# The scores of two attention steps issued together, and the turns of a step ahead of every product with V

## What is computed

```python
for layer in range(DEPTH):
    h = _rmsnorm(x, mix_norm_gain[layer])
    proj = h @ w_in[layer].astype(h.dtype)
    q, k, v, conv_in = jnp.split(
        proj, [ATTN_WIDTH, 2 * ATTN_WIDTH, 3 * ATTN_WIDTH], axis=-1)
    ...
    q = _rope(_rmsnorm(q, q_norm_gain[layer]), cos, sin)
    k = _rope(_rmsnorm(k, k_norm_gain[layer]), cos, sin)
    attn = _dilated_attention(q, k, v).reshape(b, s, ATTN_WIDTH)
    ...
    mix = jnp.concatenate([attn, u], axis=-1)
    x = x + mix @ w_out[layer].astype(mix.dtype)
    ...
    x = x + (jax.nn.silu(gate) * val) @ w_down[layer].astype(h.dtype)
```

## Time and profile before

| | |
|---|---|
| median of 3 runs | 2282.95 us (2280.68 to 2283.87) |
| profiled execution, its own time | 2281.74 us |
| its span | 2280.0 us |
| PE busy | 2237.1 us, 98% |
| DVE busy | 1791.0 us, 79% |
| ACT busy | 950.4 us, 42% |
| attention stage, layer one | about 246 to 371 us of the span |
| attention stage, layer two | about 1378 to 1503 us |

### The profile page before, as it was taken

One profiled execution on the slowest core, in us unless ns is written; L12 is line 12 of the kernel. 1 busy time (PEld: TensorE's weight loads), 2 busy tenths in 40 slices (PEclk: granted clock), 3 DMA queues, 4 the chain that ended last, 5 costly groups with the idle time before them and its releaser, 6 DMA issues.

```text
span 2280.0 us, 31670 instructions
## 1 busy us (share of the span) xinstructions
PE 2237.1 (98%) x11160; PEld 1852.5 (81%) x11160; DVE 1791.0 (79%) x2259; ACT 950.4 (42%) x1454; POOL 150.4 (7%) x65
## 2 busy tenths in 40 slices
PE   8999999999999999999999999999999999999999
PEld 6888788887888888888788887888878888888887
DVE  5999885688777777778849998856887777777785
ACT  5323685444333333333432237845533333333331
POOL 0131002100000000000102210021000000000000
PEclk9999999999999999999999999999999999999999
DMA  4324640101111111111212246401011111111112
GB/s 160 103 84 120 167 112 11 65 19 56 39 54 55 55 55 55 55 55 37 93 47 83 75 129 178 92 20 56 19 56 56 56 41 51 55 55 55 55 39 109
DMA packets 47980, 158.25 MB, mean 69 GB/s; under 512 B 7568, under 2 KB 10256, under 8 KB 47888
## 3 DMA queue, kind: packets, MB, share of 16 engines
q1 hardware_dynamic: 47024, 154.64, 21.6%
q10 hardware_dynamic: 864, 2.36, 0.3%
HBM read 135.74 MB, written 21.23 MB: 69 GB/s over the span
## 4 chain that ended last, share of the span: by engine, by line
PE 87%; DVE 8%; issue 1%; ACT 1%; DMA 1%; DVEq 0%; SPq 0%; ACTq 0%
PE mm L600 34%; PE aux L611 20%; PE mm L611 17%; PE mm L697 4%; PE aux L773 4%; PE aux L755 3%; PE mm L728 3%; PE aux L636 1%; DMA w_raw<-weights 1%; DVE cv L1895 1%; DVE y L1595 1%; DVE t_all L1941 1%; DVE ring L1873 1%; DVE x_lo L1825 1%; DVE ring L1505 0%
## 5 line engine op out<-in xcount | busy, mean ns | idle before, releaser
L600 PE MATMUL mm<-x_hi,ring 128*128 128x512 f32 x1536 | 498.6, 390 | 4.5 <-ACT uv L1336 2.9
L611 PE MATMUL aux<-hidden,ring 128*128 128x512 f32 x1920 | 439.9, 389 | 5.6 <-DVE x L1512 5.6
L611 PEld LDWEIGHTS aux<-hidden,ring 128*128 128x128 f32 x1920 | 359.8, 188 | 82.7 <-issue 8.1
L611 PE MATMUL mm<-x_hi,ring 128*128 128x512 f32 x1280 | 352.3, 393 | 10.9 <-DVE x_lo L1521 10.8
L600 PE MATMUL mm<-t_all,ring 128*128 128x512 f32 x1440 | 346.1, 389 | 2.9 <-DVE ring L1873 2.9
L600 PEld LDWEIGHTS mm<-x_hi,ring 128*128 128x128 f32 x1536 | 289.0, 188 | 66.0 <-issue 6.0
L600 PEld LDWEIGHTS mm<-t_all,ring 128*128 128x128 f32 x1440 | 270.2, 188 | 59.7 <-DVE ring L1873 3.6
L600 PE MATMUL mm<-x_lo,ring 128*128 128x512 f32 x768 | 299.3, 390 | 0.0
L611 PEld LDWEIGHTS mm<-x_hi,ring 128*128 128x128 f32 x1280 | 238.9, 188 | 60.9 <-issue 12.1
L1512 DVE TENSOR_TENSOR x<-x,aux 128x1024 f32<-128x1024 f32 x176 | 214.7, 1220 | 88.5 <-PE aux L611 88.4
L1281 ACT ACTIVATE ring<-w_raw 128x512 fp32r<-128x512 f32 x208 | 125.8, 625 | 236.5 <-PE aux L611 173.1
(11 more groups left out here) (208 smaller groups left out, 2966.2 us busy)
## 6 DMA issues: line engine op xcount, KB each, us to landing
w_raw<-weights SPq DMA_DIRECT2D x196, 512.0 KB, 3.6
qk_scratch<-m SPq DMA_DIRECT2D x64, 128.0 KB, 2.1
qk_scratch<-o SPq DMA_DIRECT2D x64, 128.0 KB, 2.1
x_hi<-qk_scratch SPq DMA_DIRECT2D x32, 256.0 KB, 6.5
ring<-qk_scratch SPq DMA_DIRECT2D x8, 512.0 KB, 4.6
ring<-qk_scratch SPq DMA_DIRECT2D x16, 256.0 KB, 6.0
k_ll_first<-qk_scratch SPq DMA_DIRECT2D x16, 256.0 KB, 6.5
x_hi<-qk_scratch SPq DMA_DIRECT2D x8, 512.0 KB, 4.7
```

Source lines behind the costliest of these rows:

```text
L600: last = pe.matmul(acc, a, b, start=start and n == 0, stop=stop and n == 2, skip_group_check=more)
L611: last = pe.matmul(acc[:, cols], a, b[:, cols], start=start and n == 0, stop=stop and n == 2)
```

## The change

In every even step PE now issues the scores of that step and of the next; in odd steps it issues none. The turns of a step now stand ahead of its product with V for every k; before, this was so for even k only. Nothing is added or removed, and the programs of DVE, ACT, POOL and SP stay as they are.

```diff
-                    if n < STEPS:
+                    if n < STEPS and n % 2 == 0:
                         scores(n)
+                        scores(n + 1)
                     if n == 0:
                         plain(pe)
                     attends = [((n - first) // TB, k) for k, (first, _, _) in enumerate(ATTENDS)
                                if (n - first) % TB == 0 and 0 <= n - first < STEPS]
-                    for h, k in attends:
-                        if k % 2:
-                            attend(h, k)
                     for f in range(PT):
                         if FILLS[f][0] == n and FILLS[f][1] == "p":
                             turn(f)
                     for h, k in attends:
-                        if k % 2 == 0:
-                            attend(h, k)
+                        attend(h, k)
                     for f in range(PT):
                         if FILLS[f][0] == n and FILLS[f][1] in "ho":
                             turn(f)
```

## The result

The changed kernel takes 2299.43 us (median of 6 runs, 2297.23 to 2299.95); the kernel before, run beside it, 2282.84 us (6 runs, 2280.68 to 2285.85). The ratio is 1.007, with a 95% interval of 1.0059 to 1.0080: 16.6 us slower. Forecast were 9.1 us and a range up to 2298.0, so the sign was right and the size too small.

What follows compares the result with a forecast made beforehand. PE was taken as the bound, with DVE and ACT some 80% busy. Per layer 2.3 + 0.9 + 0.7 + 0.6 = 4.5 us, 9.0 for both, gave 2292.0 against the median; predicted 2291.9, range 2284.5 to 2298.

Steps and rivals of the forecast that it cites:

- Slower, by waits of PE on ACT's reads behind the 11-product: Main forecast: between heads PE waits 0.26 at the 3-product and 0.23 at the "h" turn; net 2.3 us a layer.
- The slack is 0.16: At a pair's second scores: the largest mask needs 1.48 us after the turns, PE's work ahead takes 1.64.
- the rival of DVE as a bound: Odd steps' masks come 0.45 later and hold up PE's scores: 0.3 a head, 4.8 in all, 2296.8 us; chance 0.08.
- the walk: The forecast's step-by-step timing of attention work on the engines, from durations and distances in the profile's rows of the kernel before.
- the "o" turn's bank alone: Behind the 15-product, every second head: PE waits 0.37 for ACT's read, taken as 0.3, 3 times: 0.9 us a layer.
- The loss is 2.1 - 1.4 = 0.7 us: Each layer's start: first 15-product 2.1 us later, less 1.4 of scores and turns already done ahead of it.
- The end: Step 64 has no scores as cover, so its second fill waits some 0.6 us for a bank ACT reads, per layer.
- Changeovers: Turns instead of scores behind the 3- and 7-product save 0.05 twice a head: 0.1 a head, 1.6 us for 16 heads.
- The rule on batches: Back-to-back matmuls might keep the clock up: at most 1.8 us won in the first 16 us window; put at 0.
- Nothing but changeovers: Rival: no new wait lasts since ACT starts sooner after products; about 2282.8 us, 2286.6 with half the waits; chance 0.19.
- faster: Rival: PE's waits for masks at a layer's start shrink; 6.7 us gained with other gains, 2276.3 us; chance 0.07.
- DVE's case: Late masks of odd steps hold up PE's scores in every head, 0.3 a head; 2296.8 us, range up to 2298; chance 0.08.

Runs made afterwards that it cites:

- e6: Changed kernel with ACT's move of a head's result copying 8 of 512 columns; 2296.20 us (one run).
- e5: Changed kernel with DVE's split of the "o" turns subtracting 8 of 512 columns; 2292.93 us (one run).
- e4: Changed kernel with GpSimd's sums of the convolution's channels adding 8 of 1024 columns; 2299.22 us (4 runs) beside 2284.24.
- e11: The kernel before, unchanged, run and profiled once more; 2282.28 us (one run).
- e10: Changed kernel with scores one by one in the first six steps, turns between both scores in steps 6 and 8, pairs from 10; 2297.35 us beside 2284.08.
- e9: Kernel before, with only the scores of step 8h + 7 issued early, between step 8h + 6's turns and the 3-product; 2283.03 us beside 2284.08, ratio 0.9997.
- e12: Changed kernel with ACT's move, DVE's "o" split and the GpSimd sums all shortened together; 2285.46 us (one run).

## Why the prediction was right or wrong

- **Slower, by waits of PE on ACT's reads behind the 11-product.** Right in place and size. The two waits came at 2.58 and 3.78 us behind the product, forecast 2.66 and 3.86, and are 0.18 and 0.23 us, forecast 0.26 and 0.23; the distance without an "o" turn rose by 0.39, forecast 0.33. e6 shows the cause: 0.42 go when the move is short.
- **"The slack is 0.16"**, the rival of DVE as a bound at 0.08. This is the step that failed. In heads without an "o" turn the slack was used up but PE hardly waited: the mask started 0.33 behind its turns where the walk had 0.20. In the others the walk left out what stands on DVE ahead of that mask: the split of the "o" turn, which waits for ACT, which waits for the 15-product. With it PE waits 0.44 in each of these heads, and e5 takes 0.5 to 1.0 away. For the "o" heads I had costed the "o" turn's bank alone (0.3 a head); that wait came with its 0.37. And the tap that a GpSimd sum stretches to 2.4 us was absorbed before; with the slack used up it costs 0.8 a layer (e4). Together everything behind the start was forecast at 3.8 us a layer and measured 6.1.
- **The start, "The loss is 2.1 - 1.4 = 0.7 us".** It was 2.4 in layer one and 2.7 in layer two. A part of this is the clock of the two profiles: against e11, which has the same granted clock of 0.79, it is 2.0 and 1.6. The walk took every row at full clock. In the trace the scores of step 5 took 1.45 us instead of 0.79 and the turns of steps 1 and 2 took 1.78 instead of 0.99, in both layers, and the scores of step 6 took 1.0 instead of 0.5. These 1.9 us swallowed the wait of 0.78 for the mask of step 5 that the walk had. From step 5's scores to step 7's it took 4.2 us where the walk had 3.0: 1.2 of the 1.7 that were missing in layer one and of the 2.0 in layer two. In layer two the scores of step 4 came 0.5 later as well, behind their wait for the mask of step 2. The remaining 0.3 to 0.5 are smaller pieces; the scores of steps 8 and 9, which took 1.30 instead of 1.14, are one of them. The clock falls in the kernel before too (e11), and there the seven turns of step 1 show 1.70 us in layer two instead of 0.93, but waits of PE for masks stand between these pieces. I read it so that part of the loss is taken out of these waits, and that with nine turns gathered behind the last wait PE's own pace counts in full. e10, whose first six steps have the order of before, has the start of before apart from the work moved ahead. I have no profile of the paired start at full clock, so that its length there is open.
- **The end.** Forecast as a loss of 0.6 a layer, by a bank wait of 0.6. Right: PE waits 0.63 there. It is contained in the seventh distance, which rose by 0.86 though it lost the scores of a step 65, 0.9; e5 and e6 take away 0.5 and 0.4, and the wait stays.
- **Changeovers**, a gain of 0.1 a head. One place alone is worth the forecast 0.05 (e9). In the changed kernel the gain is not found: its two waits are 0.18 + 0.23 = 0.41, and less the old 0.06 that is 0.35, while the distance rose by 0.39. In e12, where these waits are gone, it is 14.53 against 14.55. The forecast counted some of the changes between kinds of work that the new order makes, and what the others cost is not isolated. One part shows: the scores of the pair 8h + 12 and 8h + 13 take 1.23 us in heads without an "o" turn, where the second start right behind their mask, and 1.15 in those with one in e12, where the mask is over sooner.
- **The rule on batches** of the Trainium skill (Perfetto Trace Analysis, Matmul Optimizations), for which I put 0: the first window's clock went from 0.89 to 0.79 in this profile, and was 0.79 in e11 without the change, so these runs show no gain from batches of scores and fit the 0.
- **Nothing but changeovers** and **faster** are out. The range failed at its upper end because that end, 2298, took in DVE's case as a plain mask that is late (0.3 a head). What else stands in the queues (2.3 us a layer behind the start, with the changeovers) and PE's pace at the start (1.7 to 2.0 a layer) were not in it.

## What to carry to other kernels

When a step is moved ahead of others on a saturated engine, walk from the moved place to every wait that follows, on every engine, with all that stands in the other queues ahead of the released work; a slack that is true for a plain step is not for the one that carries an extra instruction. Two halves of a reordering can interact by more than either is worth (25.6 and 0.7 us alone, 16 together), so run them apart. And where an engine has no idle time and the two beside it are 80% busy, do not expect much from order: here the best order of those tried saved 0.6 us a layer.

## What the runs showed of the hardware

- A product with 64 columns of weights costs 0.09 us on the way in from turns (eight turns and the changeover 0.97, in e6 and e12). On the way out it costs about 0.05 more when scores follow than when turns do: e9, which changes one such place a head, gained 0.05 where PE had not waited.
- A turn of a 128x128 block takes 0.11 us at full clock and 0.20 (1.78 / 9) at the start where the clock is halved for most of it.
- The granted clock over the first 16 us of the attention stage was 1.00 in one layer and 0.89 in the other in the first profile of the kernel before, and 0.79 in both in its second (e11), whose start is up to 1.1 us longer. Ahead of the fall PE waits for masks, busy 3.77 of 9 us in the window of e4.
- A tap of the convolution (a DVE instruction with two inputs in SBUF) takes 0.75 us elsewhere and 2.38 beside a GpSimd sum of 2.37 us.
